# First weight blocks moved from SyncE's DMA queue to ScalarE's, eight identity matmuls taken out, in a hybrid attention trunk

## What is computed

```python
h = x
for i in range(DEPTH):                      # DEPTH = 2
    hn = _rmsnorm(h, norm_mix[i])
    if i % 2 == 0: mix = _windowed_gqa(hn, positions, a_w_qkv[j], a_sink[j], a_w_o[j])
    else:          mix = _mla(hn, positions, b_w_in[j], ...)
    h = h + mix
    h = h + _swiglu(_rmsnorm(h, norm_ffn[i]), ffn_w_gu[i], ffn_w_down[i])
return _rmsnorm(h, final_norm)
```

## Time and profile before

| what | us |
|---|---|
| median of 3 runs | 1177.7 |
| lowest and highest of them | 1176.38, 1177.74 |
| the profiled execution | 1178.11 |
| span of its instructions | 1176.3 |
| TensorE busy in the span | 1146.1 (97%) |
| VectorE, ScalarE, GpSimd busy | 608.2, 361.2, 454.6 |

### The profile page before, as it was taken

How to read it: one execution, slowest core, us unless ns; L and a number is a source line. 1 busy time by engine, 2 the same in 40 slices (tenths; PEclk the granted TensorE clock), 3 DMA queues, 4 the chain that set the end, 5 groups by cost and what they waited for, 6 DMA issues and landing times.

```text
span 1176.3 us, 17004 instructions
## 1 busy us (share of the span) xinstructions
PE 1146.1 (97%) x5625; PEld 955.6 (81%) x5625; DVE 608.2 (52%) x1028; ACT 361.2 (31%) x720; POOL 454.6 (39%) x475
## 2 busy tenths in 40 slices
PE   7999999999999999999989999999999999999997
PEld 6877678788888888888978888878788888888886
DVE  5688854433424434455379888654434333343433
ACT  6288822222100111111167777522222100111102
POOL 2367744333312332344146455553333311323352
PEclk9999999999999999999999999999999999999999
DMA  7311122333432333333211001033333432333321
GB/s 189 103 42 37 36 73 82 97 89 107 117 98 72 90 106 89 112 96 95 82 39 39 17 21 36 19 108 90 94 103 91 121 91 79 100 89 107 113 84 72
DMA packets 177088, 97.78 MB, mean 83 GB/s; under 512 B 8848, under 2 KB 173200, under 8 KB 177040
## 3 DMA queue, kind: packets, MB, share of 16 engines
q1 hardware_dynamic: 177040, 97.17, 28.2%
HBM read 94.01 MB, written 2.10 MB: 82 GB/s over the span
## 4 chain that ended last, share of the span: by engine, by line
PE 89%; DVE 4%; ACT 2%; issue 2%; POOL 2%; DMA 1%; ACTq 0%; SPq 0%; DVEq 0%; POOLq 0%
PE bank L1318 27%; PE bank L1322 26%; PE bank L1321 26%; PE bank L1875 2%; PE bank L1894 1%; PE bank L1897 1%; PE bank L1479 1%; PE bank L1463 1%; POOL w_hi L502 1%; DVE w_lo L2068 1%; PE bank L1494 1%; PE bank L1825 1%; PE bank L1495 1%; DMA x_n<-in_x 1%; ACT s_a L929 0%
## 5 line engine op out<-in xcount | busy, mean ns | idle before, releaser
L2068 DVE TENSOR_TENSOR w_lo<-w_raw,w_hi 128x1024 fp32r<-128x1024 f32 (+2 forms) x142 | 191.5, 1350 | 289.2 <-POOL w_hi L502 289.1
L502 POOL TENSOR_SCALAR w_hi<-w_raw 128x1024 fp32r<-128x1024 f32 (+3 forms) x150 | 174.3, 1162 | 392.2 <-PE bank L1322 392.1
L1318 PE MATMUL bank<-x_hi,w_lo 128*128 128x512 f32 x768 | 300.6, 391 | 2.9 <-DVE gate_t L2378 1.8
L1322 PE MATMUL bank<-x_hi,w_hi 128*128 128x512 f32 x768 | 299.0, 389 | 0.0
L1321 PE MATMUL bank<-x_lo,w_hi 128*128 128x512 f32 x768 | 298.9, 389 | 0.0
L1318 PEld LDWEIGHTS bank<-x_hi,w_lo 128*128 128x128 f32 x768 | 144.2, 188 | 33.4 <-DVE gate_t L2378 2.6
L1322 PEld LDWEIGHTS bank<-x_hi,w_hi 128*128 128x128 f32 x768 | 144.2, 188 | 30.0
L1321 PEld LDWEIGHTS bank<-x_lo,w_hi 128*128 128x128 f32 x768 | 144.2, 188 | 29.5
L1318 PE MATMUL bank<-f_hi,w_lo 128*128 128x512 f32 (+1 forms) x363 | 139.9, 386 | 1.1 <-DVE f_lo L2391 1.1
L1322 PE MATMUL bank<-f_hi,w_hi 128*128 128x512 f32 (+1 forms) x363 | 139.0, 383 | 0.0
L1321 PE MATMUL bank<-f_lo,w_hi 128*128 128x512 f32 (+1 forms) x363 | 138.9, 383 | 0.0
(11 more groups left out here) (251 smaller groups left out, 1861.3 us busy)
## 6 DMA issues: line engine op xcount, KB each, us to landing
w_raw<-in_ffn_w_gu SPq DMA_DIRECT2D x88, 512.0 KB, 3.8
w_raw<-in_ffn_w_down SPq DMA_DIRECT2D x32, 704.0 KB, 4.5
w_raw<-in_a_w_qkv SPq DMA_DIRECT2D x10, 512.0 KB, 4.1
w_raw<-in_a_w_o SPq DMA_DIRECT2D x8, 512.0 KB, 3.7
w_raw<-in_b_w_o SPq DMA_DIRECT2D x8, 512.0 KB, 3.7
w_raw<-in_b_w_in SPq DMA_DIRECT2D x4, 672.0 KB, 4.1
w_raw<-in_b_w_uq SPq DMA_DIRECT2D x4, 576.0 KB, 4.0
x_n<-in_x SPq DMA_DIRECT2D x4, 512.0 KB, 5.4
```

The source lines that it names most:

```text
L502: pool.tensor_scalar(split_part(w_hi, s, cols, kv), raw_part(s, cols, kv), 1.0, 1.0, ALU.mult, ALU.mult) \
L1318: first = pe.matmul(o, ll, rh, start=start, stop=False)
L1322: return pe.matmul(o, lh, rh, start=False, stop=stop)
L2068: dve.tensor_tensor(split_part(w_lo, s, cols, kv), raw_part(s, cols, kv), f(split_part(w_hi, s, cols, kv)), ALU.subtract) \
```

## The change

SyncE no longer issues the first two weight blocks. ScalarE issues them, after a wait for the first piece of `x` and ahead of its first square. The eight identity matmuls and the two waits ahead of them are removed. The first key product has waits of its own on the same two semaphores.

```diff
             load_gain(0, norm_mix[0], gain_in)
-            load(0, 0, qkv_v[:, :, 8, :], P)
-            load(0, 1, qkv_v[:, :, 9, :], P)
             for i in range(2):
                 sp.dma_start(q01_raw[i][:]..., qkv_v[:, :, i, :]).then_inc(q01_in[i], 16)
...
+            act.wait_ge(x_in[0], 16)
+            for s in range(2):
+                act.dma_start(w_raw[s][:, 0:W_COLS].rearrange("p (k n) -> p k n", n=P), qkv_v[:, :, 8 + s, :]) \
+                    .then_inc(w_in[s], 16)
             x_square(0)
             x_square(1)
             x_square(2)
...
-            pe.wait_ge(h_act, 1)
-            pe.wait_ge(x_ready, 1)
-            for i in range(8):
-                pe.matmul(banks[6][:, 0:P], ident[:], ident[:], start=True, stop=True)
             for s in range(2):
                 for pos in range(KD // 2):
                     k_block(pos, s)
```

## The result

The changed kernel takes 1179.41 us (median of 12 runs, 1178.18 to 1180.13), the kernel before 1177.0 us (median of 12, 1175.35 to 1177.79). The ratio is 1.0019, with a 95% interval of 1.0010 to 1.0028: slower by 2.2 us by the ratio and by 2.4 us by the medians. The difference is measurable, and 1179.41 lies inside the borders of the prediction, 1175.3 and 1180.1. The profiled execution took 1178.48 us with a span of 1176.7, only 0.4 more than the 1176.3 of before.

A forecast was written before the change was run, and what follows sets the result against it. TensorE was taken to bound the kernel, busy 1146.1 of 1176.3 us. An earlier first key product (-0.6) and a clock fall (+1.5) gave +0.9 us, 1178.6 for the median, with a range of 1175.6 to 1182.4.

The forecast's parts named there:

- the class: Outcome predicted against the kernel before: within 0.2% (2.4 us), borders 1175.3 and 1180.1, chance 0.55.
- the forecast's own range: Total time of 1176.8 to 1180.3 us, from an early start without clock loss to a start at 14.8 with it.
- The two issues on ScalarE: Head, ScalarE's queue: issuing both weight blocks takes 1.09 us each, with 0.37 and 4.84 as the ends.
- The first x_hi at 11.2: Head, ScalarE: first x_hi moves from 10.27 to 11.2, as weights sharing the DMA engines delay x and gain by 0.9.
- Rival B: Head: ScalarE's second issue waits for SyncE's until 9.2; +3.6 to +4.4 us, 1181.7 taken, chance 0.34.
- Rival A: Head: transfers don't hurt each other, issues are short, the clock holds; -1.8 us, 1175.9, chance 0.12.
- Rival C: Head: weights land no earlier (11.7), first key product at 13.45; 1176.8 to 1178.3, chance counted within the forecast's 0.48.
- the one on the query blocks: SyncE's queue: query blocks move up two places, share with the weights and land no later; nothing on the path.
- The first key product: Head, TensorE: starts at 13.7 instead of 14.32, a gain of 0.6 us, bounds 12.5 and 14.8.
- The clock: TensorE, head: a pause of 2.5 us makes the granted clock fall to 0.50; 1.5 us charged, between 0 and twice that.
- I let a shift of the head pass in full: Head to end: a shift reaches the total in full, up to 2.1 us where only TensorE gains.
- Its own sign: Check at the end of the key products, 25.3 before: it should carry the whole difference in time.

The follow-up runs named there:

- a_hold: The changed kernel with one more wait on SyncE, so the two query blocks are issued only when the last piece of x has landed: 1177.23 us.
- a_fill: The changed kernel with 24 further transposes of the last square of x into bank 3, so TensorE doesn't pause before the first key product: 1179.49 us.
- a_remove: The kernel before without the eight identity matmuls, all loads as before: 1177.36 us, ratio 1.0004.
- b_fill: The kernel before with 18 further transposes into bank 3 in place of the identity matmuls: 1177.75 us, ratio 1.0009.
- a_move: The changed kernel with the eight identity matmuls put back, so only the loads are moved: 1178.14 us, ratio 1.0013.

## Why the prediction came out right, and where it was wrong

The range (1175.6 to 1182.4) and the class (within 0.2%) held, and the forecast of 1178.6 was 0.8 below the time; against the kernel before it said +0.9 where +2.4 was measured by the medians and +2.1 heap against heap. That the time came so near is in part luck: of the three runs known of the kernel before, two were in the upper heap, and their median of 1177.7 lay 0.7 above that of twelve runs. The upper end of the forecast's own range, 1180.3, doesn't come out of its terms either: 1177.7 + 0.5 + 1.5 = 1179.7. Point by point:

- **The two issues on ScalarE**: forecast 2.18 us together, measured 2.26. The sum is right, by luck: the two took 0.44 and 1.79 and not 1.09 each. The first x_hi at 11.2: measured 11.20. Right in its size and half in its reason, since x lost nothing (its slowest piece took 7.4 us from issue to landing, and 7.5 before), while the gain took 8.6 us where it had taken 7.5, and was the last thing awaited, by 0.35. In a_hold, where it shares with the weights and no query block stands behind it, it took 7.9.
- **Rival B**, ScalarE's issue waiting for SyncE's: fell. The changed kernel's trace alone doesn't settle it, since there ScalarE's second issue began before SyncE's second. In a_fill it began behind it, at 4.59, and was over at 6.54, while SyncE's lasted to 9.41. The rule of the Trainium skill ("Perfetto Trace Analysis", DMA Instruction — HWDGE (DVE, Sync)), an exclusive lock until all descriptors are written, would have held ScalarE there until 9.4 if SyncE's lock lasts as long as its issue; the measurement decides, and ScalarE was not held.
- **Rival A**, nothing hurts the other: fell. **Rival C**, the weights land no earlier: true, and the change is worse than that. The step that failed first is the one on the query blocks. The prediction let the weights share with x and the gain and asked what x loses; it put the queries down as harmless ("they land no later than the sum of all bytes did before", "Nothing there is on the path") and didn't ask whom they hurt. They had stood behind the weights and now stood beside them, and the weights landed 1.3 and 3.2 us late. a_hold shows it with one wait.
- **The first key product**: forecast 13.7, measured 14.80, last released by w_lo and not by the copy. It lies on the edge of the stated bounds (14.8). The sum had no term for late weights: the copy, which it had as the last thing awaited, was done at 13.40, and the half of w_lo only at 14.74.
- **The clock**: forecast a fall that costs 1.5; it fell, for 6.8 us, of which 5.5 were key products, and cost the keys 2.6 (3.1 less the 0.5 of the start). That it fell was right, and the term was mis-sized by 1.1. That the length of the pause decides, as the prediction had it, is not shown: the clock fell at the start of the keys in a_remove, behind a pause of 2.86 us, and held in a_hold, behind one of 3.02.
- **"I let a shift of the head pass in full"**: wrong, and the most useful miss. rs_n was given as 2.1 us early, and so it is for TensorE's spread. But GpSimd waits for rs_n as well, and VectorE's work behind the keys is stretched while GpSimd is busy. Earlier keys were worth nothing or half (a_remove, b_fill), later keys were swallowed up to 1 us, and a later rs_n counted one for one. The prediction read the wait that ended last at 25.33 and not who else waited for the same result. Its own sign said that the end of the key products should carry the whole difference; they ended 3.1 us late, which is 0.9 more than reached q_tmp.

Summed by its own steps, the forecast was -0.6 + 1.5 = +0.9; measured in the trace it is +0.5 + 2.6 - 0.9 = +2.2 along TensorE and +2.0 to +2.1 along rs_n. The two paths agree by accident. The forecast is off by 1.3: the start of the keys by 1.1 and the clock by 1.1, less the 0.9 that the passing in full left out.

## What to carry to other kernels

When a transfer is taken out of a queue, look at what moves up into its place: two queues that were both full had 51.6% and 51.5% of the DMA engines' time here, and a block that waited behind the urgent one now runs beside it. Before a pause of an engine is priced, follow each result that the head makes to all its readers, and see which instructions of a third engine are stretched beside another one's. Where the time has two heaps, compare executions instruction by instruction and set the heaps aside, since a change of 2 us is drowned by a fall of the clock that comes in one execution and not in the next.

## What the runs showed of the hardware

- The fall of the clock isn't set by the length of the pause alone. It fell behind pauses of 1.98 us (before, at 764.6) and 1.4 us (a_hold, before 42.6), and held behind one of 3.0 us in the head of a_hold. Near 765 TensorE pauses for 1.97 to 1.99 us in all twelve executions; in five the clock fell there, at a cost of about 1.5 us, and in seven it didn't.
- An fp32 or int32 instruction of VectorE on data in SBUF took 1.23 us beside GpSimd and 0.28 without it (the first CAST), ks_lo for two blocks 2.33 and 1.49. The Trainium skill ("SBUF — State Buffer", Who interferes with whom) tells of a port pair that the two engines share and that blocks the loser for a whole instruction. The numbers here fit that: the CAST lost 0.95 us, and one rounding of GpSimd beside it takes 1.04 (two take 2.08). No run here rules out another cause of the stretching.
- On a queue of its own, a weight block issued at 4.04 had moved no byte by 8 us, by the packets of the trace:

```profile
q1 hardware_dynamic: 521, 1.24, 92.2%
```

(Queue, packets, MB and share from 4 to 8 us; ScalarE's queue, q10 on the page of the changed kernel, isn't among them. In a_fill and a_move it has moved nothing by 8 us either, in a_hold four packets.) From 8 to 12 us both queues had half:

```profile
q1 hardware_dynamic: 1620, 0.47, 51.6%
q10 hardware_dynamic: 1126, 0.57, 51.5%
```

Why the second queue gets nothing while x is under way was not tried and stays open. That it gets nothing until then goes with there being nothing to win: in a_hold, where ScalarE's queue then had the DMA engines nearly to itself, the weights landed when they do from SyncE's.
